# A two-layer decoder trunk on one core: RMS norm applied after the input projections, and a different wait and VectorE order in the retention stage

## The reference, cut to what matters

```
h   = rms_norm(x, norm1_g)                 # x * rsqrt(mean(x*x) + 1e-6) * gain, per token
p   = h @ w_in                             # 1024 -> 2560, split among the head groups
y_r = silu(r_g) * rms_norm(retention(rotary(r_q), rotary(r_k), r_v), ret_norm_g)
y_m = moba_attention(rms_norm(m_q), rms_norm(m_k), m_v)
kv  = rms_norm(mem, mem_norm_g) @ w_mem_kv # mem is 256 x 1024
y_c = memory_attention(rms_norm(c_q), rms_norm(kv[:, :256]), kv[:, 256:])
x   = x + concat(y_r, y_m, y_c) @ w_out
x   = x + hier_moe(rms_norm(x, norm2_g))   # 16 experts, each token goes to two
```

## Time and profile before

| | |
|---|---|
| median of three runs | 1183.69 us |
| profiled execution, its own time | 1185.31 us |
| its span | 1183.4 us |
| mean granted TensorE clock | 0.971 of full speed |
| PE busy | 1096.7 us (93%) |
| DVE busy | 897.9 us (76%) |
| ACT busy | 714.6 us (60%) |
| chain that ended last, by engine | PE 78%, DVE 13%, DMA 4%, issue 3%, ACT 1% |
| share of that chain in the three matmul lines of `three` | 64% |

### The profile page before, as it was taken

One profiled execution on the slowest core, in us unless ns is written; L12 is line 12 of the kernel. 1 busy time (PEld: TensorE's weight loads), 2 busy tenths in 40 slices (PEclk: granted clock), 3 DMA queues, 4 the chain that ended last, 5 costly groups with the idle time before them and its releaser, 6 DMA issues.

```text
span 1183.4 us, 18042 instructions
## 1 busy us (share of the span) xinstructions
PE 1096.7 (93%) x5562; PEld 913.5 (77%) x5562; DVE 897.9 (76%) x1310; ACT 714.6 (60%) x999; POOL 164.5 (14%) x238
## 2 busy tenths in 40 slices
PE   4999999999999999999569999989999999999990
PEld 3887887788788888888458878878878888888870
DVE  5459676647989999999394586674689999999973
ACT  6334432324888888888352354432378888888860
POOL 2000312001010110110400005110011012011111
PEclk9999999998999999999789999999999999999995
DMA  9532111208999979999763221202299996999965
GB/s 344 183 90 70 55 54 63 89 36 289 374 380 381 361 265 384 379 382 348 292 206 97 71 89 55 79 20 107 99 368 377 379 374 251 372 374 385 386 239 223
DMA packets 121872, 277.26 MB, mean 234 GB/s; under 512 B 13265, under 2 KB 13473, under 8 KB 121680
## 3 DMA queue, kind: packets, MB, share of 16 engines
q1 hardware_dynamic: 106912, 240.30, 55.9%
q0 software_dynamic: 14896, 36.19, 8.3%
HBM read 269.56 MB, written 23.07 MB: 247 GB/s over the span
## 4 chain that ended last, share of the span: by engine, by line
PE 78%; DVE 13%; DMA 4%; issue 3%; ACT 1%; POOL 0%; POOLq 0%; DVEq 0%; SPq 0%; ACTq 0%
PE bank L1451 22%; PE bank L1453 21%; PE bank L1452 21%; PE bank L1804 2%; PE bank L1483 2%; DVE w_lo L411 2%; PE bank L1603 1%; PE bank L1823 1%; PE bank L1597 1%; DMA hd<-pair_rows 1%; PE bank L1707 1%; PE bank L1661 1%; DVE x L970 1%; DMA xg<-h_scratch,slot_tok 1%; PE bank L1754 1%
## 5 line engine op out<-in xcount | busy, mean ns | idle before, releaser
L407 DVE TENSOR_TENSOR w_lo<-stage,w_hi 128x1024 fp32r<-128x1024 f32 x244 | 293.6, 1219 | 11.8 <-ACT w_hi L402 3.7
L402 ACT ACTIVATE w_hi<-stage 128x1024 fp32r<-128x1024 f32 x236 | 246.4, 1059 | 44.3 <-PE bank L1453 38.7
L1451 PE MATMUL bank<-w_hi,hT_hi 128*128 128x512 f32 x384 | 156.9, 409 | 4.6 <-DVE hT_lo L984 4.5
L1453 PE MATMUL bank<-w_hi,hT_lo 128*128 128x512 f32 x384 | 151.1, 393 | 0.0
L1452 PE MATMUL bank<-w_lo,hT_hi 128*128 128x512 f32 x384 | 150.7, 392 | 0.0
L407 DVE TENSOR_TENSOR more_lo<-stage,more_hi 128x1024 fp32r<-128x1024 f32 x124 | 146.1, 1217 | 3.1 <-ACT more_hi L402 2.1
L402 ACT ACTIVATE more_hi<-stage 128x1024 fp32r<-128x1024 f32 x124 | 127.9, 1061 | 15.5 <-PE bank L1453 12.3
L411 DVE TENSOR_TENSOR w_lo<-stage,w_hi 128x1024 fp32r<-128x1024 f32 x56 | 67.6, 1219 | 56.2 <-ACT w_hi L370 54.9
L370 ACT ACTIVATE w_hi<-stage 128x1024 fp32r<-128x1024 f32 x56 | 58.7, 1055 | 82.6 <-PE bank L1453 82.6
L1451 PE MATMUL bank<-w_hi,xgT_hi 128*128 128x512 f32 x264 | 103.9, 393 | 1.1 <-DVE xgT_lo L1351 1.1
L1453 PE MATMUL bank<-w_hi,xgT_lo 128*128 128x512 f32 x264 | 103.8, 393 | 0.0
(11 more groups left out here) (263 smaller groups left out, 2031.0 us busy)
## 6 DMA issues: line engine op xcount, KB each, us to landing
stage<-in_w_exp_up SPq DMA_DIRECT2D x124, 512.0 KB
stage<-in_w_exp_gate SPq DMA_DIRECT2D x122, 512.0 KB
stage<-in_w_exp_down SPq DMA_DIRECT2D x122, 512.0 KB
stage<-in_w_in SPq DMA_DIRECT2D x40, 512.0 KB
stage<-in_w_out SPq DMA_DIRECT2D x16, 512.0 KB
stage<-in_w_mem_kv SPq DMA_DIRECT2D x8, 512.0 KB
h_scratch<-act POOLq DMA_DIRECT2D x8, 512.0 KB, 3.2
act<-pair_rows POOLq DMA_DIRECT2D x8, 512.0 KB, 6.4
```

The source lines that it names most:

```text
L402: eng.activation(x_hi[n % NX], src, ACT.Copy).then_inc(s_hi, 1)
L407: eng.tensor_tensor(x_lo[n % NX], src, x_hi[n % NX].bitcast(f32), ALU.subtract).then_inc(s_lo, 1)
L1451: pe.matmul(dst, l_hi, r_hi, start=start, stop=False)
L1453: return pe.matmul(dst, l_lo, r_hi, start=False, stop=stop)
```

## The change

1. `make_hi` and `make_lo` multiply the 24 projection units of a layer by the gain of their input feature. The gain is a per-partition scalar, and a unit holds two feature tiles, so each becomes two instructions of 128 x 512. `g_cols` holds the gains of both norms and both layers as columns; it is made once, from two small loads (16 rows of 128 values each), one PE transpose and a DVE copy.
2. The two 512 KB gain loads of each layer on POOL are gone.
3. The memory rows and `x` are transposed as they are. The squares of all six tiles and one square root come behind the `x` banks on ACT, one reciprocal behind them on DVE; the token's factor `rstd` is the `scale` of the copies of the memory product (`ck`, `cv`) and of `evacuate`.
4. DVE no longer norms. In its place `split_x(t-1)` (one weight unit, two banks) stands directly behind the arrival (layer 0) or sum (layer 1) of tile `t`.
5. On PE the transposes of the last `x` tile move from before `project(0)` to behind its first two row tiles, and the PSUM banks of the `x` transposes change.
6. Retention: `s_yev` is waited for only ahead of the fourth transposed tile; DVE's clear of `state` and the scaling of `qdT` move behind the masks of the second pair; `ret_squares(0)` moves behind the masks of the seventh pair.

```diff
-        g_norm1 = hd[:, 0, :, :].rearrange("p g c -> p (g c)")
+        g_rows = early[0:2 * DEPTH * KT, 0, 0:128]
+        X_BANK = (6, 7, 2, 3, 6, 7, 6, 7)
+        def halves(layer, n):
+            which = 0 if n < U_MEM else 1
+            for kk in range(2):
+                k = 2 * (n % 4) + kk
+                yield slice(512 * kk, 512 * kk + 512), g_cols[:, which, layer, k:k + 1]
...
-            eng.activation(w_hi[:, n % NW, :], stage[:, n % NS, :], ACT.Copy).then_inc(s_hi, 1)
+            if n < U_MEM + U_PROJ:
+                for part_, gain in halves(layer, n):
+                    ins = eng.activation(w_hi[:, n % NW, part_], stage[:, n % NS, part_], ACT.Copy, scale=gain)
...
+            if n < U_MEM + U_PROJ:
+                for part_, gain in halves(layer, n):
+                    ins = eng.scalar_tensor_tensor(out=w_lo[:, n % NW, part_], in0=stage[:, n % NS, part_], scalar=gain,
+                                                   in1=w_hi[:, n % NW, part_].bitcast(f32),
+                                                   op0=ALU.mult, op1=ALU.subtract)
...
+            for which, name in enumerate(("mem_norm_g", "norm1_g")):
+                rows_ = slice(DEPTH * KT * which, DEPTH * KT * (which + 1))
+                sp.dma_start(g_rows[rows_, :], a[name].rearrange("l (k p) -> (l k) p", p=128)).then_inc(s_first_c, 16)
...
-                pool.dma_start(gvec[:, :], row(a["mem_norm_g"])).then_inc(s_gain[0], 16)
-                pool.dma_start(g_norm1, row(a["norm1_g"])).then_inc(s_gain[1], 16)
...
-                sc.wait_ge(s_memx, p * 16 + 16)
-                for t in range(2):
-                    squares(mem_rows[:, t, :], t)
-                root(rstd[:, 0:2], ss[:, 0:2], D, s_std)
...
-                for t in range(NT):
-                    sc.wait_ge(s_x, layer * 16 + 4 * (t + 1))
-                    squares(x[:, t, :], 2 + t)
-                    root(rstd[:, 2 + t:3 + t], ss[:, 2 + t:3 + t], D, s_std)
                 for k in range(4):
                     make_hi(sc, base, 4 + k)
...
+                sc.wait_ge(s_memx, p * 16 + 16)
+                apart(sc)
+                for t in range(2):
+                    squares(mem_rows[:, t, :], t)
+                sc.wait_ge(s_x, layer * 16 + 16)
+                for t in range(NT):
+                    squares(x[:, t, :], 2 + t)
+                root(rstd[:, 0:6], ss[:, 0:6], D, s_std)
+                sc.wait_ge(s_h1, 1)
                 for t in range(2):
                     sc.wait_ge(s_used, base[0] + (U_MEM + NW))
-                    sc.activation(ck[:, t, 0:256], bank[4 + t][:, 0:256], ACT.Copy)
+                    sc.activation(ck[:, t, 0:256], bank[4 + t][:, 0:256], ACT.Copy, scale=rstd[:, t:t + 1])
...
-                dv.wait_ge(s_std, 1)
-                chain(dv.reciprocal(rstd[:, 0:2], rstd[:, 0:2]))
-                dv.wait_ge(s_gain[0], layer * 16 + 16)
-                for t in range(2):
-                    norm(mem_rows[:, t, :], mem_rows[:, t, :], t, s_hm, gvec[:, :])
...
+                def split_x(k):
+                    make_lo(dv, base, layer, 4 + k)
+                    for j in (2 * k, 2 * k + 1):
+                        bank_lo(4 + j, X_BANK[j], hT_part(hT_lo, j), hT_part(hT_hi, j))
...
                     if t:
-                        norm_x(t - 1)
-                norm_x(NT - 1)
-                for k in range(4):
-                    make_lo(dv, base, 4 + k)
-                    for j in (2 * k, 2 * k + 1):
-                        bank_lo(4 + j, (6, 7, 0, 1, 2, 3, 6, 7)[j], hT_part(hT_lo, j), hT_part(hT_hi, j))
+                        split_x(t - 1)
+                split_x(NT - 1)
+                dv.wait_ge(s_std, 1)
+                dv.reciprocal(rstd[:, 0:6], rstd[:, 0:6]).then_inc(s_h1, 1)
...
-                chain(dv.memset(state, 0.0))
-                dv.tensor_tensor(qdT, hd[:, 0, :, 256:512], qdec, ALU.mult).then_inc(s_qd, 1)
...
+                    if r == 1:
+                        chain(dv.memset(state, 0.0))
+                        dv.tensor_tensor(qdT, hd[:, 0, :, 256:512], qdec, ALU.mult).then_inc(s_qd, 1)
...
+                    if r == 6:
+                        ret_squares(0)
...
-                for j in range(4):
-                    pe.wait_ge(s_hm, j // 2 + 1)
...
+                        if n == j == 0:
+                            for t in range(NT):
+                                if t == 2:
+                                    turn_in(3)
+                                rows(hT_hi, hT_lo, base, 4, 0, (0, 1, 2, 3), only=t, split=(6, 8, 10, 12))
...
-                pe.wait_ge(s_yev, 4)
                 pe.wait_ge(s_rot, 1)
                 for j in range(4):
+                    if j == 3:
+                        pe.wait_ge(s_yev, 4)
                     turn(lambda q: pq[0][:, q, 128 * j:128 * j + 128], j, s_tq)
```

More of the change, by code:

```diff
@@ L238, in build @@
         s_memx = sem("s_memx")
-        s_gain = [sem(f"s_gain{i}") for i in range(4)]
+        s_gain = {i: sem(f"s_gain{i}") for i in (2, 3)}
         s_small = sem("s_small")
@@ L1004, in _ @@
                 for n in range(2, 4):
-                    make_lo(dv, base, n)
-                dv.wait_ge(s_gain[1], layer * 16 + 16)
-                apart(dv)
-                def norm_x(t):
-                    dv.wait_ge(s_std, 2 + t)
-                    chain(dv.reciprocal(rstd[:, 2 + t:3 + t], rstd[:, 2 + t:3 + t]))
-                    norm(act[:, t, :], x[:, t, :], 2 + t, s_h1, g_norm1)
+                    make_lo(dv, base, layer, n)
+                def split_x(k):
+                    make_lo(dv, base, layer, 4 + k)
+                    for j in (2 * k, 2 * k + 1):
+                        bank_lo(4 + j, X_BANK[j], hT_part(hT_lo, j), hT_part(hT_hi, j))
                 for t in range(NT):
@@ L1068, in _ @@
                 for k in range(4):
-                    make_lo(dv, base, 8 + k)
+                    make_lo(dv, base, layer, 8 + k)
                 for t in range(NT):
@@ L1074, in _ @@
                 for k in range(4):
-                    make_lo(dv, base, 12 + k)
+                    make_lo(dv, base, layer, 12 + k)
                 dv.wait_ge(s_stdq, 1)
@@ L1154, in _, with ret_squares @@
                 dv.wait_ge(s_tqe, 14)
-                chain(dv.memset(state, 0.0))
-                dv.tensor_tensor(qdT, hd[:, 0, :, 256:512], qdec, ALU.mult).then_inc(s_qd, 1)
+                def ret_squares(c):
+                    for t in (2 * c, 2 * c + 1):
+                        dv.wait_ge(s_rsq, t + 1)
+                        dv.tensor_reduce(ssr[:, 4 * t:4 * t + 4], sqr[:, t % 2, :].rearrange("p (h c) -> p h c", h=H),
+                                         axis=AX.X, op=ALU.add).then_inc(s_ssr, 1)
                 for r in range(8):
@@ L1443, in _ @@
             pe.sem_inc(s_used, NW)
-            pe.wait_ge(s_first_c, 16)
+            pe.wait_ge(s_first_c, 48)
+            n_rows = 2 * DEPTH * KT
+            pe.transpose(bank[7][:, 0:n_rows], g_rows, ident[0:n_rows, 0:n_rows]).then_inc(s_cols_t, 1)
             passes = pe.alloc_register("pe_passes")
@@ L1494, in _, with turn_in @@
                 rows(mT_hi, mT_lo, base, 0, 0, (4, 5))
-                for k in range(4):
-                    if k < 3:
-                        rows(mT_hi, mT_lo, base, k + 1, k + 1, (4, 5))
-                    pe.wait_ge(s_h1, k + 1)
+                def turn_in(k):
+                    pe.wait_ge(s_x, layer * 16 + 4 * (k + 1))
                     for j in (2 * k, 2 * k + 1):
-                        if j >= 6:
-                            pe.wait_ge(s_trl, 4 + j - 5)
-                        turn(lambda q: act[:, k, 512 * (j % 2) + 128 * q:512 * (j % 2) + 128 * q + 128],
-                             (6, 7, 0, 1, 2, 3, 6, 7)[j], s_tr)
+                        if j >= 4:
+                            pe.wait_ge(s_trl, 4 + (j - 3 if j < 6 else j - 1))
+                        turn(lambda q: x[:, k, 512 * (j % 2) + 128 * q:512 * (j % 2) + 128 * q + 128], X_BANK[j], s_tr)
+                for k in range(3):
+                    rows(mT_hi, mT_lo, base, k + 1, k + 1, (4, 5))
+                    turn_in(k)
                 def project(n):
@@ L1510, in project @@
                     for j in range(4):
-                        rows(hT_hi, hT_lo, base, 4 + 4 * n + j, j, tuple(range(4 * (n % 2), 4 * (n % 2) + 4)),
-                             split=(8, 8, 10, 12) if n == j == 0 else None,
-                             done=s_proj)
+                        if n == j == 0:
[3 more added lines that the diff above has]
+                                rows(hT_hi, hT_lo, base, 4, 0, (0, 1, 2, 3), only=t, split=(6, 8, 10, 12))
+                        else:
+                            rows(hT_hi, hT_lo, base, 4 + 4 * n + j, j, tuple(range(4 * (n % 2), 4 * (n % 2) + 4)),
+                                 done=s_proj)
                 project(0)
```

58 lines of the change are left out of this document (34 added, 24 removed).

## The result

Nine runs of the changed kernel gave a median of 1179.68 us (1175.16 to 1181.91), nine of the kernel before beside them 1187.12 us (1182.32 to 1188.83). The ratio is 0.9943, with the interval 0.9928 to 0.9957: about 7 us faster, a third of the 20.8 us forecast, and 8.7 us above the end of the range. The profiled execution took 1175.16 us, span 1173.2 us, the fastest of its nine. Compared with the profiled one of before it is 10.2 us shorter, some 3 us more than the ratio gives. Its mean granted clock was 0.977, against 0.970 to 0.975 in the eight others and 0.971 in the profiled run of before, which fits this excess but does not prove it.

A forecast was written before the change was run, and what follows sets the result against it. PE, busy 93% of the span, was taken as the bound, so only its standstills could be won. Terms 6.0 + 10.8 + 4.6 - 0.6 = 20.8 us gave about 1163 us, with an 8-in-10 range of 1156 to 1171.

The forecast's parts named there:

- four terms: Whole kernel: start of layer 0 6.0 us, start of layer 1 10.8, retention 4.6, less 0.6 for the dearer split.
- the rivals: Other outcomes: transfers hold layer starts (0.11), retention moves nothing (0.09), ACT's block outlasts its cover (0.04), clock takes gain back (0.04).
- Start of layer 0: Kernel start: first projection matmul at 13.4 us instead of 19.76, with unit 1 landing about 9; gain 6.0 us, ends 3.5 and 7.5.
- Start of layer 1: Layer boundary: memory projection at 587 us, last `hT_lo` near 611, `project(0)` ending 10.8 us earlier; ends 7 and 12.5.
- The block moved to ACT: Behind the `x` banks: some 11 us of ACT work, covered by PE's 22 us of `project(0)`; rival of 5 us overrun per layer, 0.04.
- The signs named ahead: Disproof by ACT waiting on `stage` before 12 us, DVE's sums waiting for `pair_rows`, or a 1.2 GHz clock row beyond 625.
- The dearer split: Projection weight units split as two halves: 0.08 us more each on DVE, costing 0.3 us per layer, 0.6 in all, ends 0 and 1.5.
- Retention: Retention stage: earlier first transposes and gates bring the output projection 2.3 us earlier per layer, 4.6 in all, ends 2 and 6.
- The clock: Rival in `project(0)`: holes keep PE at 1.2 GHz, giving 1180 us (one layer) or 1196 (both); chance 0.04, half of it slower.
- A slip in a rival: Retention rival: its loop is PE's, so the 4.6 us fall away; with the split by the skill's formula 1168.4 us; chance 0.09.

The follow-up runs named there:

- The run with both put right: Changed kernel with gains in free parts of tiles, gain loads moved to ACT's queue and an early dummy activation for the table load: 1171.99 us, ratio 0.9871.
- the last kernel: Changed kernel with gains in free parts of tiles, gain loads on ACT's queue, early table load and 64 unused bytes ahead of `ss`: 1165.79 us, ratio 0.9838.
- the kernel without the shift: Changed kernel with its gain columns kept in free parts of `prod` and `lg`, so every tile keeps its old address: 1173.55 us, ratio 0.9894.

## Why the prediction was wrong

The step that failed is "Behind `project(0)` PE is the bound in both layers, and what it starts earlier is carried on to the end ... Hence the sum is made of four terms". PE is the bound there, and just for that reason the pace of its matmuls was a term of the sum. The prediction put it at nothing and gave no reason. The traces show 3.9 and 3.7 us more in the two expert stages, 7.6 of the 10.6 us that are missing, from a shift of 128 bytes: shown by the shift alone, by taking it away, for one tile alone and with other distances. By the medians the shift is worth a little less, 6.5 us alone and 5.8 between the changed kernel and the one without it. None of the rivals held it either; the diff, though, did: a new tile in the middle of the allocations.

Point by point, by the working on record:

- **Start of layer 0**, forecast 6.0, measured 3.9 at the end of `project(0)` and 3.6 at the first projection matmul (19.76 to 16.19), near the low end of 3.5. I looked for the landing of unit 1 and not of unit 0. ACT waited for unit 0 until 8.25; with the table load, which the order showed at this place and which I priced only where it had been, the chain of ACT and DVE started 1.3 us later still. From ACT's 9.55 on it went as worked out: four halves, then the banks. The run with both put right shows that unit 1, which I placed at "about 9", is used at 10.12, and that alone makes 15.43, not 13.4. In the last kernel, with the same start, unit 1 is used at 9.72 and the projection starts at 15.04.
- **Start of layer 1**, forecast 10.8, measured 10.4: the size is right, but two errors cancel in it. The memory projection starts at 584.49, 6.5 us behind the transposes (forecast 6.3 behind 580.7); the last `hT_lo` comes at 609.44, and ends 32.7 us behind them, where 30.2 was forecast, with 2.6 us of waiting for `pair_rows` in it, where 0.6 was allowed. What made this good is the clock: I charged 2.6 us for matmuls of `project(0)` at 1.2 GHz, as before until 622.90, and in this trace its matmuls start about 0.23 us apart from 610.8 on, with a clock share of 1.00 in every stretch from 600. So that charge did not fall due. The stretch before ends earlier by what the layer gained, which is why the times themselves lie ahead of the forecast's.
- **The block moved to ACT** had its cover. In layer 1 its root comes at 617.80, and no wait of PE for unit 8 appears.
- **The signs named ahead.** Two of the three that were to prove the prediction wrong did show: ACT waited for `stage` until 8.25 us, and DVE's sums waited for `pair_rows`. A clock row at 1.2 GHz beyond 625 did not. None of the three looked at the experts' stage.
- **The dearer split**, forecast 0.3 a layer, measured 1.6 and 1.9. The run with the split alone confirms it. This term was sized wrong in two ways. Two halves take DVE 1.41 us (0.19 more, not 0.08), since I read the price of a half from a subtraction of a PSUM bank; and ACT's halves take 1.33 where the whole took 1.06, which I had left out though ACT works ahead of DVE on every unit.

```profile
29.88 1.41 DVE L428 SCALAR_TENSOR_TENSOR w_lo<-stage,g_cols,w_hi 128x512 fp32r<-128x512 f32 x2 [0.42 <-ACT w_hi L382]
...
54.82 1.34 ACT L382 ACTIVATE w_hi<-stage,g_cols 128x512 fp32r<-128x512 f32 x2 [4.10 <-PE bank L1480]
56.06 2.40 ACT L770 ACTIVATE proj<-bank,rstd 128x512 f32<-128x512 f32 x4
```

  The rule of the Trainium skill (VectorE: DVE Perf Modes, "The TRN2 errata"), a fixed latency for each instruction, was the better guide: its 0.16 us lies near the 0.19 measured. The last row shows the scaled copies of `evacuate` at 0.60 each; in the grouped view they have a median of 683 ns against 596 before, within the 0.1 us that I had allowed.
- **Retention**, forecast 2.3 a layer, measured 2.4 and 2.5: right, and alone it gives the same in the trace.
- **The clock** took nothing back on balance. Its share rose from 0.82 to 0.87 at the layer boundary and from 0.93 to 0.95 between retention and experts in layer 0; in layer 1 it fell there, from 0.98 to 0.95. The rows -2.0, +1.3 and -1.4 of the table, 2.1 us in all, go the same way as these shares and that of the end (0.63 to 0.67), and nothing in the change acts there. That the clock made them is argued from this, not tested.
- **A slip in a rival**: with retention at nothing and the split by the formula, the time is 1183.7 - 16.8 + 0.6 + 1.5 = 1169.0 us; the record has 1168.4, without the 0.6.

The sum: 20.8 forecast, less 7.6 (pace), 2.9 (split), 2.1 (start of layer 0), 0.4 (layer 1), and 0.3 and 2.1 more (retention, the rest): 10.2, as the profiled pair shows. Without the pace and without the last 2.1, 15.7 us remain for the kernel without the shift, where its ratio gave 12.6. That difference of 3 us is open, as is why retention alone gave 7.8. Both are of the size of what the clock changes between runs: the stretch from the output projection to the first `silu` of layer 1, the same work in all of them, took 74.1 us before at a clock share of 0.98, and 78.9 without the shift and 79.5 with retention alone, both at 0.91.

## What to carry to other kernels

Where one engine is the bound for hundreds of us, its pace is a term of every sum: compare the number of instructions and the length of such a stretch first, and look in the diff for tiles that are added, since they move others. A tile for a few scalars belongs in a free corner of another, as was tried here, or behind the operands of matmuls, which was not. When one instruction is cut in two, price both engines that work on the piece, from rows with the same operands.

## What the runs showed of the hardware

The spacing of matmuls of 512 f32 columns back to back at full clock went with the distance in bytes, within a partition, between the stationary and the moving operand, here modulo 256 (which fits all runs; a longer period is not excluded). The distances are worked out from the order and sizes of the allocations, the spacings (lowest and highest mean of a pair of tiles) from the traces:

```
stationary - moving, mod 256    ns between starts      seen on
  0                             226.8 to 229.6         xgT, hidT with 64 bytes; wx there 227.2 to 228.4; hT with w 227.5 to 228.9
192                             226.9 to 230.9         xgT, hidT before and without the shift; wx with hT after 227.0 to 231.8
 64                             233.0 to 233.8         xgT, hidT after and with 128 bytes; wx with hT before 233.3 to 234.1
224                             232.4 to 233.7         xgT, hidT with 32 bytes
 32                             233.2                  wx with hT with 32 bytes
```

Five distances are too few for a rule, two of them (32 and 224) come from a single run, and what in the chip makes the difference was not tested. Between best and worst lie 3%, which no wait, no busy share and no granted clock shows.
